# Second block's norm transitions: GpSimd scales six of eight tiles by the root, and VectorE writes the first tile's rounded half itself

## The reference

```python
h = h + 0.5 * rmsnorm(swiglu(rmsnorm(h, g_pre_ffn1[l]), ...), g_post_ffn1[l])
h = h + rmsnorm(mix, g_post_mix[l])            # mix = token_mixer(rmsnorm(h, g_pre_mix[l]), ...)
h = h + 0.5 * rmsnorm(swiglu(rmsnorm(h, g_pre_ffn2[l]), ...), g_post_ffn2[l])
```

## Time and profile before

| what | value |
|---|---|
| median of 3 runs | 2322.44 us (2321.61 to 2323.95) |
| the profiled execution | 2326.09 us, of it span 2324.3 us |
| TensorE busy | 2271.7 us, 98% of the span |
| VectorE busy | 1556.9 us, 67% |
| ScalarE busy | 1202.8 us, 52% |
| GpSimd busy | 150.2 us, 6% |

### The profile page before, as it was taken

The page is one execution under the profiler, slowest core; times in us unless marked ns, Lnnn a source line. Parts: engine busy times, 40 slices in busy tenths (PEclk is TensorE's granted clock), DMA queues, the critical chain, the costliest instruction groups (busy, mean ns, idle before and its releaser), DMA issues.

```text
span 2324.3 us, 46182 instructions
## 1 busy us (share of the span) xinstructions
PE 2271.7 (98%) x17075; PEld 2080.1 (89%) x17075; DVE 1556.9 (67%) x2775; ACT 1202.8 (52%) x2060; POOL 150.2 (6%) x246
## 2 busy tenths in 40 slices
PE   7998999999999999999999999999999999999998
PEld 5786788888878789999999989999999999899998
DVE  5556678887777568866656846676466558466764
ACT  5547444443236656654445565644454455656553
POOL 0226200000110410000000000000000000000000
PEclk9999999999999999999999999999999999999999
DMA  9740234435645025565555424455645554254654
GB/s 340 228 171 1 92 108 162 144 135 162 196 138 153 19 84 189 179 182 166 179 170 157 137 94 151 139 192 171 177 150 178 168 157 137 92 174 152 199 183 124
DMA packets 103166, 356.41 MB, mean 153 GB/s; under 512 B 11392, under 2 KB 15136, under 8 KB 103040
## 3 DMA queue, kind: packets, MB, share of 16 engines
q1 hardware_dynamic: 89248, 306.55, 41.3%
q0 software_dynamic: 13792, 48.14, 6.5%
HBM read 352.55 MB, written 1.05 MB: 152 GB/s over the span
## 4 chain that ended last, share of the span: by engine, by line
PE 91%; DVE 3%; ACT 3%; issue 2%; DMA 1%; POOL 0%; DVEq 0%; ACTq 0%; SPq 0%
PE ps L828 25%; PE ps L830 25%; PE ps L829 25%; PE ps L845 1%; PE ps L849 1%; PE ps L986 1%; PE ps L846 1%; PE ps L1021 1%; PE ps L1005 1%; DMA ada_rest<-in_w_ada 1%; PE ps L916 1%; PE ps L1356 1%; PE ps L1314 1%; PE ps L1285 1%; ACT probs L1502 1%
## 5 line engine op out<-in xcount | busy, mean ns | idle before, releaser
L1964 DVE TENSOR_TENSOR wl<-raw,wh 128x1024 fp32r<-128x1024 f32 x571 | 697.8, 1223 | 395.2 <-ACT wh L1448 394.7
L828 PE MATMUL ps<-hH,wh 128*128 128x272 f32 (+2 forms) x2880 | 886.5, 308 | 4.1 <-DVE silu L2714 3.1
L829 PE MATMUL ps<-hL,wh 128*128 128x272 f32 (+2 forms) x2880 | 875.5, 304 | 0.0
L830 PE MATMUL ps<-hH,wl 128*128 128x272 f32 (+2 forms) x2880 | 875.2, 304 | 0.0
L1448 ACT ACTIVATE wh<-raw 128x1024 fp32r<-128x1024 f32 x571 | 599.7, 1053 | 305.1 <-PE ps L830 289.1
L828 PEld LDWEIGHTS ps<-hH,wh 128*128 128x128 f32 x2880 | 544.0, 189 | 32.6 <-DVE silu L2714 4.0
L829 PEld LDWEIGHTS ps<-hL,wh 128*128 128x128 f32 x2880 | 544.0, 189 | 20.3 <-issue 0.2
L830 PEld LDWEIGHTS ps<-hH,wl 128*128 128x128 f32 x2880 | 543.7, 189 | 19.9
L830 PE MATMUL ps<-actH,wl 128*128 128x272 f32 (+2 forms) x1184 | 358.5, 303 | 0.0
L828 PE MATMUL ps<-actH,wh 128*128 128x272 f32 (+2 forms) x1184 | 356.5, 301 | 0.2 <-ACT actH L1618 0.2
L829 PE MATMUL ps<-actL,wh 128*128 128x272 f32 (+2 forms) x1184 | 356.4, 301 | 0.0
(11 more groups left out here) (320 smaller groups left out, 2836.4 us busy)
## 6 DMA issues: line engine op xcount, KB each, us to landing
raw<-in_w_ffn_gu SPq DMA_DIRECT2D x176, 512.0 KB, 3.5
raw<-in_w_mix SPq DMA_DIRECT2D x98, 512.0 KB, 3.5
raw<-in_w_up SPq DMA_DIRECT2D x88, 512.0 KB, 3.6
raw<-in_w_ffn_down SPq DMA_DIRECT2D x64, 512.0 KB, 3.5
ada_rest<-in_w_ada POOLq DMA_DIRECT2D x32, 512.0 KB, 4.8
raw<-in_w_out SPq DMA_DIRECT2D x32, 512.0 KB, 3.9
raw<-in_w_down SPq DMA_DIRECT2D x32, 512.0 KB, 3.5
weights_a<-in_w_ada POOLq DMA_DIRECT2D x24, 512.0 KB, 3.7
```

Source lines behind the costliest of these rows:

```text
L828: pe.matmul(out, a_h, b_h, start=start, stop=False)
L829: pe.matmul(out, a_h, b_l, start=False, stop=False)
L830: return pe.matmul(out, a_l, b_h, start=False, stop=stop)
L1964: dve.tensor_tensor(wl[:, slot, :], raw[:, slot, :], wh[:, slot, :].bitcast(F32), ALU.subtract).then_inc(l_split, 1)
```

## The change

- GpSimd gets `scale_far`: in each transition it writes `nh32` for tiles 2 to 7, each with a semaphore step (`post_far`), once the root is there. At post_ffn1 it stands behind the three table loads and ahead of the memsets. In `last_norm` it scales the pairs 2 and 3.
- VectorE scales tiles 0 and 1 alone, and waits for `post_far` ahead of each added(2) to added(7).
- hH of tile 0 is written by VectorE. Before the root it makes `gained = h * gain` (a 128x272 tile, in a buffer that TensorE has done with), and behind scaled(0) it writes hH[0] = nh32 * gain + gained. ScalarE then does only the square of tile 0.
- ScalarE's wait between Ln and Exp goes over a semaphore that is there already, in place of `ln_ready`.

```diff
+            def scale_far(p):
+                pool.wait_ge(root_ready, p.idx + 1)
+                for k in range(2, KT):
+                    pool.tensor_tensor(p.nh32[:, k, p.lo:], y2[:, k, p.lo:], p.rstd, ALU.mult).then_inc(post_far, 1)
...
+                scale_far(norms["post_ffn1", l])        # behind the table loads
                 pool.wait_ge(x_tile, 8 * post_before[norms["post_ffn1", l].idx] + 8)
...
+                scale_far(norms["post_mix", l])
+                p = norms["post_ffn2", l]
+                if l == 0:
+                    scale_far(p)
+            pool.wait_ge(root_ready, p.idx + 1)
+            rstd = p.rstd.unsqueeze(1).to_broadcast([P, 2, TX])
+            for q in (2, 3):
+                pool.tensor_tensor(p.nh32[:, 2 * q:2 * q + 2, p.lo:], y2[:, 2 * q:2 * q + 2, p.lo:], rstd,
+                                   ALU.mult).then_inc(post_far, 1)
...
-                act.activation(n.rstd, ps[:, 5, n.lo:n.T], ACT.Ln, bias=eps_col[:]).then_inc(ln_ready, 1)
-                act.wait_ge(ln_ready, n.idx + 1)
+                link(act.activation(n.rstd, ps[:, 5, n.lo:n.T], ACT.Ln, bias=eps_col[:]))
...
-                act.activation(hH[:, k, n.lo:T2], xs(k, n.lo), ACT.Copy, scale=col(n.which, n.layer, k)).then_inc(hh_ready, 1)
+                if k or n.post is None:
+                    act.activation(hH[:, k, n.lo:T2], xs(k, n.lo), ACT.Copy,
+                                   scale=col(n.which, n.layer, k)).then_inc(hh_ready, 1)
...
+                dve.wait_ge(ss_ready, p.idx + 1)
+                dve.tensor_scalar(gained, xs(0, p.lo), gain, None, ALU.mult)
                 dve.wait_ge(root_ready, p.idx + 1)
...
                 def added(k):
-                    dve.wait_ge(post_t, g0 + k + 1)
+                    if k < 2:
+                        dve.wait_ge(post_t, 2 * post_before[p.idx] + k + 1)
+                    else:
+                        dve.wait_ge(post_far, f0 + k - 1)
                     dve.tensor_tensor(xs(k, p.lo), p.nh32[:, k, p.lo:], xs(k, p.lo), ALU.add).then_inc(x_tile, 1)
 
                 scaled(0)
+                dve.wait_ge(post_t, 2 * post_before[p.idx] + 1)
+                dve.scalar_tensor_tensor(hH[:, 0, n.lo:T2], p.nh32[:, 0, p.lo:], gain, gained, ALU.mult,
+                                         ALU.add).then_inc(hh_ready, 1)
                 added(0)
                 scaled(1)
-                for k in range(1, KT):
-                    if k + 1 < KT:
-                        scaled(k + 1)
+                added(1)
+                rest(n, 0)
+                for k in range(2, KT):
                     added(k)
-                    if n:
-                        rest(n, k - 1)
+                    rest(n, k - 1)
```

More of the change, by code:

```diff
@@ L432, in build_program @@
         post_t = sem("post_t")
-        ln_ready = sem("ln_ready")
+        post_far = sem("post_far")
         z_psum = sem("z_psum")
@@ L1992, in add_square, with transition @@
                     link(ins)
-            def transition(p, n=None, st=None):
-                g0 = 8 * post_before[p.idx]
+            def transition(p, n, st):
+                g0, f0 = 8 * post_before[p.idx], (KT - 2) * post_before[p.idx]
+                gain = col(n.which, n.layer, 0)
+                gained = p.nrstd[:, 0, p.lo:]
+                dve.wait_ge(ss_ready, p.idx + 1)
+                dve.tensor_scalar(gained, xs(0, p.lo), gain, None, ALU.mult)
                 dve.wait_ge(root_ready, p.idx + 1)
@@ L2002, in added @@
                 def added(k):
-                    dve.wait_ge(post_t, g0 + k + 1)
+                    if k < 2:
+                        dve.wait_ge(post_t, 2 * post_before[p.idx] + k + 1)
+                    else:
+                        dve.wait_ge(post_far, f0 + k - 1)
                     dve.tensor_tensor(xs(k, p.lo), p.nh32[:, k, p.lo:], xs(k, p.lo), ALU.add).then_inc(x_tile, 1)
                 scaled(0)
+                dve.wait_ge(post_t, 2 * post_before[p.idx] + 1)
+                dve.scalar_tensor_tensor(hH[:, 0, n.lo:T2], p.nh32[:, 0, p.lo:], gain, gained, ALU.mult,
+                                         ALU.add).then_inc(hh_ready, 1)
                 added(0)
                 scaled(1)
-                for k in range(1, KT):
-                    if k + 1 < KT:
-                        scaled(k + 1)
+                added(1)
+                rest(n, 0)
+                for k in range(2, KT):
                     added(k)
-                    if n:
-                        rest(n, k - 1)
+                    rest(n, k - 1)
                 dve.wait_ge(x_tile, g0 + KT)
                 dve.sem_inc(x_ready, 1)
[L2017 to L2023, removed]
+                rest(n, KT - 1)
+                split(st, Step(0, 0, RING))
+                for _ in range(KT - 2):
+                    add_square(n)
+                split(st, Step(0, 1, RING))
+                dve.wait_ge(root_ready, n.idx + 1)
             def last_norm(p):
@@ L2034, in last_norm @@
                 scaled(0)
+                scaled(1)
                 for q in range(4):
-                    if q < 3:
-                        scaled(q + 1)
                     t = slice(2 * q, 2 * q + 2)
-                    dve.wait_ge(last_scaled, q + 1)
+                    if q < 2:
+                        dve.wait_ge(last_scaled, q + 1)
+                    else:
+                        dve.wait_ge(post_far, (KT - 2) * post_before[p.idx] + q - 1)
                     dve.tensor_tensor(xT[:, t, X0:T1], p.nh32[:, t, p.lo:], xT[:, t, X0:T1], ALU.add).then_inc(last_pair, 1)
```

## The result

The changed kernel takes 2349.70 us (median of 4 runs, 2346.62 to 2351.16) against 2323.02 us: ratio 1.0116, 95% interval 1.0104 to 1.0128. It is 26.7 us slower; 11.9 us were forecast, with a range up to 2339.5 us. The direction was right, the size was not.

A forecast was written before the change was run, and what follows sets the result against it. TensorE, busy 98% of the span, was taken as the bound, so only stalls at stage borders could move. 3 x 2.0 + 2 x 2.3 + 1.3 = 11.9 us on 2322.4 gave 2334.3 us, range 2326 to 2339.5.

The forecast's parts named there:

- turns, with hH on VectorE: In each transition, VectorE and GpSimd delaying each other, with tile 0's hH moved to VectorE: 2.0 us later per transition.
- run of six behind the loads: At post_ffn1, multiplies behind the table loads were to cost 0.3 us more per transition; no uninterrupted block was forecast.
- fall of the clock: TensorE's granted clock falling to 0.50 in transitions: left out of the sum, at 1.5 us per fall if it came.
- last norm: In the last norm, VectorE and GpSimd colliding: last output transfer 1.3 us later, or 0.9 if GpSimd gets in between.
- rival 3: In transitions, TensorE idling 1 to 2 us longer may lower the clock, 1.5 us each; three or more over 2339 us; 6%.
- the extra at post_ffn1: At post_ffn1, multiplies start late behind three table loads: 0.3 us more, 2.3 us per transition instead of 2.0.
- GpSimd's multiply: GpSimd's 128x272 multiply in a transition: taken as 0.72 us, between 0.67 and 0.79; 0.60 by the skill's figure.
- The collision: In transitions, VectorE ends 0.30 us behind GpSimd's multiply; waiting GpSimd gets in only at VectorE's gaps, ending 0.60 us behind it.
- one more tile must be waited for, 0.3 us: At post_ffn1, GpSimd misses the gap behind scaled 0 because table loads end 1.5 us behind R: 0.3 us more.
- taken alike: At post_ffn1 of layer 1, table loads assumed to end as in layer 0, 1.5 us behind R.
- hH on VectorE: Tile 0's hH in a transition: TensorE can start 0.57 us sooner, but hL ends at R+2.58 instead of R+2.38.
- Rival 1: No collision in transitions or last norm: 5 x 0.2 us and 1.2 us gained, 2320.2 us, faster by 0.1%; 8%.

The follow-up runs named there:

- e3: The changed kernel with more filler matmuls on TensorE in four transitions, where it stood still; 2340.50 us, ratio 1.0076 to the kernel before the change.
- e9: The changed kernel with GpSimd's multiplies ahead of the table loads at post_ffn1 and 11 more filler matmuls in each transition; 2335.72 us, ratio 1.0049 to the original.
- e1: The changed kernel with GpSimd's part undone: VectorE scales all tiles and still writes hH of tile 0; 2325.73 us, ratio 1.0011 to the original.
- e10: The changed kernel with GpSimd copying y2 into nh32 for tiles 2 to 7 instead of multiplying, so one operand is read; 2328.91 us, one run.
- e2: The changed kernel with hH of tile 0 written by ScalarE again, GpSimd's multiplies kept; 2342.72 us, ratio 1.0084 to the original.
- e6: The changed kernel with GpSimd's multiplies ahead of the table loads at post_ffn1; 2344.97 us, one run.
- e7: The changed kernel with GpSimd's multiplies waiting for VectorE's hH of tile 0 besides the root; 2343.88 us, one run.
- e11: The changed kernel with three small loads ahead of GpSimd's multiplies also at post_mix and post_ffn2 of layer 0; 2351.97 us, one run.
- e4: The changed kernel with GpSimd writing zeros by memset in place of its multiplies, so without reading; 2322.16 us, ratio 0.9996 to the original.
- e5: The changed kernel with GpSimd scaling only tiles 6 and 7 in a transition, VectorE the others; 2338.33 us, ratio 1.0046 to the original.
- e8: The changed kernel with VectorE's scaled 0 waiting for GpSimd's first multiply, so that GpSimd starts first; 2351.40 us, one run.

## Why the prediction was wrong, point by point

The late sums of the changed kernel, e3, e9 and before split the loss of 24.8 us in the transitions, and the last norm comes on top:

| term | worked out from | measured us | forecast us |
|---|---|---|---|
| turns, with hH on VectorE | e9 less before | 12.3 | 10.0 |
| run of six behind the loads | e3 less e9 | 3.1 | 0.6 |
| fall of the clock | changed less e3 | 9.4 | 0 |
| last norm | changed less before | 0.9 | 1.3 |

*The step that failed* is the clock, which the sum holds at nothing and which stands only as rival 3. I had the row of a fall before me, said that a transition with TensorE idle 1 to 2 us longer may bring one at 1.5 us each, and gave it 6%, though my own working already had TensorE lose 1.0 us at the first hL in every transition. It fell in all five, for 3.4 or 6.8 us, and cost 1.0 to 2.5 us each: 9.4 us. Waits near the 1.0 us of my working passed without a fall in e1 (0.74 us) and e10 (1.12 and 1.17 us), and with one twice in e2 (1.15 us, and as much ahead of hH); the waits of 2.5 to 5.0 us here come from who goes first, a step that I also had wrong (below). The clock doesn't make up the whole miss: e3, without the falls, is still 1 us above the range, and the rest is the run of six. Without both, e9 is 11.4 us slower by its ratio, where my terms without the extra at post_ffn1 give 11.3 (by its trace the same rows add up to 13.2).

*GpSimd's multiply.* 0.72 us was taken, and 4.34 us for six is 0.72. The other ends, 0.67 and 0.79, were not needed, and the estimate of 0.60 us was too small.

*The collision.* Right in kind: VectorE's operation ends 0.3 us behind GpSimd's. Wrong in who goes first. I read from the earlier trace rows that a waiting GpSimd gets in only where VectorE leaves a gap. At 214.06 us it is as I read it, but there GpSimd's operation is a TENSOR_SCALAR; for the multiply the trace shows strict turns, 1.0 and 0.9 us for six VectorE operations in a row, back to back or not. The Trainium skill, "SBUF — State Buffer", section "Who interferes with whom", says that whoever issues first gets the shared pair of ports for the whole instruction. The turns agree with that; the run of six behind the loads is not explained by it. I had worked the turns out too, with hL of tile 0 at R+4.7; it came at 5.06, and with fillers they cost 2.5 us per transition where I had 2.0 and 2.1. That my 2.0 came near is partly luck: I had hL of tile 0 at R+3.37 and most of the delay at the later tiles, while the trace has the delay at the front. The last remainder came out right all the same (worked out R+11.55, measured R+11.75).

*Post_ffn1.* The step "one more tile must be waited for, 0.3 us" was wrong by a factor of five. There are no turns behind the loads: VectorE waits for all six, 1.9 us (layer 0) and 1.4 us (layer 1) worse than turns. Layer 1 was "taken alike", but there the loads end at R+0.48 and not at 1.54. That it takes loads directly ahead of the multiplies is shown by e6, e7 and e11; why they have this effect is not, nor whether another instruction than a load would do the same.

*hH on VectorE.* Forecast: TensorE 0.57 us sooner, hL 0.2 us later. Measured in e1: 0.50 sooner, 0.42 later (there scaled 2 stands ahead too), and 0.41 us on the late sum, because this operation lengthens the queue that the late sum waits for. In my sum it was inside the transition's 2.0 us.

*Rival 1* was the wrong case but right in size: e4, which takes the reads away, has the remainder of tile 0 at R+2.57 (worked out 2.58), the late sum at 13.26 (13.3) and the last norm at 3.70 (3.7).

*Last norm.* 0.93 us, the 0.9 of the case with turns, not 1.3.

## What to carry to other kernels

Before work is moved from VectorE to GpSimd, look whether both read SBUF at the same time: here 0.72 us of GpSimd made a VectorE operation that was next on the path 0.5 us longer and took only 0.36 us off its queue, so every tile moved was a loss; the tiles late in the queue, where VectorE waits for ScalarE anyhow, saved nothing (e5). When a forecast makes TensorE stand still a microsecond longer, price the granted clock as a term of the sum and not as a tail; here fillers placed where the wait is (behind the matmuls that came early) gave it back. Releasing TensorE's first matmul sooner was worth nothing here, as the queue that feeds the next ones got longer by it.

## What the runs showed that I had not expected

- Multiplies that started directly behind loads which GpSimd itself issues ran as an uninterrupted block of six (4.3 us), and a VectorE operation of 0.43 to 0.50 us took 4.5 to 5.0 us (3.8 in e8, where it came in later). Without such loads, or 0.65 us behind them (e7), the two engines took turns (six multiplies in 5.2 to 5.7 us), even when GpSimd started alone (e8). This held for the multiply in every transition of every kernel here; the copy of e10 broke it once.
- In the transitions every wait of TensorE of 1.9 us and more for hL, and of 4.1 us and more for hH, was followed by a fall of the clock. Between 1.0 and 1.6 us for hL it went both ways: falls in e8's third (1.54 us, with 1.96 ahead of hH), in e5 (1.32 and 1.30) and in e2 (1.15 twice, with as much ahead of hH); none in e5's fifth (1.26), in e10 (1.17 and 1.12) or in e2's fifth (1.07). 2.15 us for hH (e10) brought none.
- Each of these falls lasted 3.4 or 6.8 us, and the length can differ for the same code: at the third transition, alike in both, 6.8 us in the changed kernel and 3.4 in e6. There is one profile per kernel, so what a single transition gains or loses by this is not to be read as an effect of an edit.
- A memset by GpSimd beside VectorE's two-operand operations costs nothing (0.43 to 0.50 us, e4), and six of them take 1.66 us.
